# Second mixer of a two-layer diffusion trunk: the chunk states are stepped group by group inside the input projection, whose column tiles come in another order

## The reference: what is computed

```python
proj = h @ in_w                                   # 1024 x (2048 + 3072 + 64)
z = proj[..., :SSD_D_INNER]
xbc = jax.nn.silu(_dwconv(proj[..., SSD_D_INNER:SSD_D_INNER + SSD_XBC], conv_w, conv_b))
dt_raw = proj[..., SSD_D_INNER + SSD_XBC:]
...
chunk_states = jnp.einsum('bcsgn,bcsgrp->bcgrpn', bm, xdt * decay_end[..., None])
...
def step(s, inp):
    st, dec = inp
    return s * dec[..., None, None] + st, s
```

## Time and profile before

| | |
|---|---|
| median of 3 runs | 3976.86 us (3973.53 to 3977.45) |
| the profiled execution | 3977.04 us, its span 3975.4 us |
| busy share | PE 88%, weight loads 74%, DVE 46%, ACT 32%, POOL 11% |
| dt projection done, rates begin | 1880.5 us from the span's start |
| last matmul of the projection | 2400.1 us |
| first transfer of the stage of its own | 2417.8 us |
| first transfer of the scan | 2568.8 us |

### The profile page before, as it was taken

The page is one execution under the profiler, slowest core; times in us unless marked ns, Lnnn a source line. Parts: engine busy times, 40 slices in busy tenths (PEclk is TensorE's granted clock), DMA queues, the critical chain, the costliest instruction groups (busy, mean ns, idle before and its releaser), DMA issues. The chain is left out here.

```text
span 3975.4 us, 58612 instructions
## 1 busy us (share of the span) xinstructions
PE 3486.9 (88%) x23815; PEld 2930.3 (74%) x23815; DVE 1821.3 (46%) x2973; ACT 1286.6 (32%) x2031; POOL 435.2 (11%) x411
## 2 busy tenths in 40 slices
PE   4999798978599999995999995679997499999995
PEld 2999543457599999994999994345554499999994
DVE  6233456455433333334204553778885533333332
ACT  4222302024132333334113332156664123333222
POOL 0000000000111111110000112400000011111121
PEclk6999898989799999996999997789997599999997
DMA  6566302154688788863222227786664478887884
GB/s 223 181 199 205 125 0 71 44 185 140 246 291 288 277 291 294 288 235 99 91 84 68 83 68 222 271 307 223 223 228 157 172 277 289 294 290 279 295 294 166
DMA packets 381736, 801.33 MB, mean 202 GB/s; under 512 B 20663, under 2 KB 65404, under 8 KB 380171
## 3 DMA queue, kind: packets, MB, share of 16 engines
q1 hardware_dynamic: 348876, 710.85, 50.6%
q0 software_dynamic: 28368, 86.61, 7.4%
q10 hardware_dynamic: 4368, 2.20, 0.3%
HBM read 690.69 MB, written 108.90 MB: 201 GB/s over the span
## 5 line engine op out<-in xcount | busy, mean ns | idle before, releaser
L2016 PEld LDWEIGHTS moe_banks<-moe_xt,mix_ring 128*128 128x128 f32 x8192 | 1012.1, 191 | 5.5 <-issue 3.2
L2016 PE MATMUL moe_banks<-moe_xt,mix_ring 128*128 128x144 f32 x8192 | 1013.4, 287 | 3.1 <-ACT moe_xt L2051 3.1
L62 PE MATMUL ssdin_banks<-h_leading,ssdin_w_split 128*128 128x384 f32 x1920 | 386.1, 336 | 5.8 <-ACT ssdin_pad L2320 2.9
L2038 PE MATMUL moe_banks<-moe_down_parts,moe_hid_parts 128*128 128x512 f32 x1536 | 357.5, 392 | 0.0
L62 PEld LDWEIGHTS ssdin_banks<-h_leading,ssdin_w_split 128*128 128x128 f32 x1920 | 337.3, 188 | 7.2 <-issue 7.2
L2096 DVE TENSOR_TENSOR moe_hid<-moe_banks,moe_sg 128x128 f32<-128x128 f32 x256 | 74.6, 292 | 580.7 <-ACT moe_sg L2074 580.7
L2038 PEld LDWEIGHTS moe_banks<-moe_down_parts,moe_hid_parts 128*128 128x128 f32 x1536 | 285.8, 188 | 71.4 <-issue 13.2
L2086 DVE TENSOR_TENSOR moe_down_parts<-mix_ring,moe_down_parts 128x2048 fp32r<-128x2048 f32 x128 | 292.3, 2283 | 0.0
L1983 POOL DMA_INDIRECT x_dram<-moe_yc,mix_idx_quarter x128 | 167.5, 1308 | 1089.3 <-DVE moe_yc L2107 1027.0
L2872 PE MATMUL scan_banks<-scan_w,scan_yc 128*128 128x512 f32 x576 | 255.9, 598 | 0.0
L62 PE MATMUL hyin_banks<-h_leading,hyin_w_split 128*128 128x384 f32 x1152 | 237.9, 338 | 11.5 <-DVE hyin_w_split L751 11.5
(11 more groups left out here) (413 smaller groups left out, 4445.4 us busy)
## 6 DMA issues: line engine op xcount, KB each, us to landing
mix_ring<-in_moe_w_gate SPq DMA_DIRECT2D x64, 2048.0 KB, 8.0
mix_ring<-in_moe_w_up SPq DMA_DIRECT2D x64, 2048.0 KB, 12.9
mix_ring<-in_moe_w_down SPq DMA_DIRECT2D x64, 2048.0 KB, 17.3
early_ring<-in_ada_w SPq DMA_DIRECT2D x96, 512.0 KB, 6.1
scan_cum<-row_dram SPq DMA_DIRECT2D x36, 1024.0 KB, 6.2
ssd_w<-in_ssd_in_w SPq DMA_DIRECT2D x10, 2048.0 KB, 9.3
scan_states<-s_dram SPq DMA_DIRECT2D x36, 512.0 KB, 7.7
s_dram<-st_state SPq DMA_DIRECT2D x16, 1024.0 KB, 10.0
```

Of the source, the lines that this page charges most:

```text
L62: ins = pe.matmul(out(piece), w_at(w[a], k), h_k(h[b], k, piece), start=(k == 0 and a == 0 and b == 0), stop=(k == KD - 1 and a == 1))
L2016: ins = pe.matmul(pb[:, 2 * (f % 2) + j, 0:SLOTS], ring[:, 2 * half + j, k, col:col + P], xt[:, k, :], start=(k == 0), stop=(k == KD - 1))
L2038: ins = pe.matmul(pb[:, LAT_BANK[half], :], hid_parts[:, a, k, :], wd[:, half, b, k, :], start=(k == 0 and a + b == 0), stop=(k == KD - 1 ...
```

## The change

`phase_states` is gone. The projection's tiles come in another order: three z tiles (q = 0 to 2), then four periods of nine, one for each group g: B (j = 0), four x tiles (j = 1 to 4), four z tiles (j = 5 to 8); in the last period C tiles take the place of three z tiles, and the fourth C tile comes last (q = 39). Each tile's 72 matmuls are cut in two halves, and small pieces of other work, called units, stand on PE behind each half (`middle`, `end`): turns of the tile before, of the initial states, and from j = 6 on two steps of both directions a tile. Units take turns in the two banks 6 and 7 that the projection leaves free. x and B are turned from SBUF, not read back. The decays are on DVE. The rates' turns and sums are spread over tiles 1 to 4. Every loop is written out; weights are loaded one tile at a time in a ring of three. The buffers of the softplus are reused for rows and states (`work`). Rows and states are stored by SP in pieces of one group. SP, ACT, PE, DVE and POOL have one program each, as before.

```diff
-def product3(pe, out, w, w_at, h, h_k):
...
+    for k in ks:
...
+TILES_IN = 40
+LEAD_IN = 3
+PERIOD = 9
+STEPS = 7
+CTX_SLOT = 7
...
+def place(q):
+    return divmod(q - LEAD_IN, PERIOD)
+def xbc_tile_of(q):
+    if q < LEAD_IN:
+        return None
+    g, j = place(q)
+    if g == GROUPS:
+        return Z_TILES + 2 * GROUPS - 1
+    if j == 0:
+        return Z_TILES + g
+    if j <= 4:
+        return 4 * g + j - 1
+    if g == GROUPS - 1 and j >= 6:
+        return Z_TILES + GROUPS + j - 6
+    return None
+def z_tile_of(q):
+    return q if q < LEAD_IN else LEAD_IN + 4 * place(q)[0] + place(q)[1] - 5
+def tile_columns(q):
+    x = xbc_tile_of(q)
+    at = z_tile_of(q) * P if x is None else INNER + x * P
...
+def ssd_weight(sp, io, keep, q):
+    win = io["ssd_in_w"][0].rearrange("(k p) n -> p k n", p=P)
+    sp.dma_start(keep["ssd_w"][:, q % SSD_RING, :, :], win[:, :, tile_columns(q)]).then_inc(keep["s_ssd_w"][q % SSD_RING], 16)
...
+U_TURN, U_LAST, U_DECAY, U_ROWS, U_GROUP, GROUP_UNITS = 0, 2, 3, 9, 12, 33
+U_B, U_X, U_INIT, U_STEP = 0, (3, 7, 11, 14), (6, 10), 17
...
+        xrow = work[:, 0:TILES * GW].rearrange("p (t c) -> p t c", c=GW)
+        state = work[:, TILES * GW:TILES * GW + 4 * GW].rearrange("p (d b c) -> p d b c", d=2, b=2)
         ROW_PARTS = ((0, 4), (4, 8), (8, 9))
+        PARTS = ((1, 5), (5, 9), (0, 1))
...
+        def side(u):
+            return pb[:, 6 + u % 2, :]
+        def wait_empty(eng, u):
+            if u >= 2:
+                eng.wait_ge(s_side[u % 2], u // 2)
...
+                def keep_step(g, i):
+                    for d in range(2):
+                        wait_taken(sp, step_unit(g, i, d))
+                        sp.dma_start(io["s_dram"][2 + i if d == FWD else 7 - i, :, g, d, :], state[:, d, (i + 1) % 2, :]
+                                     ).then_inc(s_kept[d][(i + 1) % 2], 16)
...
+                load_init(0)
+                load(SSD_RING)
+                load(SSD_RING + 1)
+                for q in range(TILES_IN):
+                    if q >= LEAD_IN:
+                        g, j = place(q)
+                        if 3 <= j <= 4:
+                            keep_init(g, j - 3)
+                        if j == 5 and g + 1 < GROUPS:
+                            load_init(g + 1)
+                        if j == 6:
+                            keep_rows(g)
+                        if j >= 6:
+                            keep_step(g, 2 * (j - 6))
+                            keep_step(g, 2 * (j - 6) + 1)
+                        if j == 0 and g:
+                            keep_step(g - 1, 6)
+                            keep_ctx(g - 1)
...
+                def turn(q, u, part):
+                    pe.wait_ge(s_si, XBC_BEFORE[q] + 1)
+                    wait_empty(pe, u)
+                    for n, c in enumerate(range(*PARTS[part])):
+                        ins = pe.transpose(side(u)[:, n * P:(n + 1) * P], out[:, q % 2, columns(c)], ident)
+                    ins.then_inc(s_unit, 1)
...
+                def contribute(g, s):
+                    if s == 0:
+                        for part in range(3):
+                            wait_taken(pe, unit(g, U_B + part))
+                    for d in range(2):
+                        u = step_unit(g, s, d)
+                        b_rows = brow[:, chunk_of(s, d), :]
+                        pe.wait_ge(s_xw, 16 * g + 2 * s + d + 1)
+                        wait_empty(pe, u)
+                        if s == CTX_SLOT:
+                            for j in range(4):
+                                ins = pe.matmul(side(u)[:, j * P:(j + 1) * P], xw[:, d, j * P:(j + 1) * P], b_rows,
+                                                start=True, stop=True)
+                        else:
+                            ins = pe.matmul(side(u), b_rows, xw[:, d, :], start=True, stop=True)
+                        ins.then_inc(s_unit, 1)
...
+                def middle(q):
+                    if q == 2:
+                        turn_last()
+                    if q == 3:
+                        cumulate(2)
+                        cumulate(3)
+                    if q == 4:
+                        for n in range(3):
+                            cumulate_rows(n)
+                    if q <= LEAD_IN:
+                        return
+                    g, j = place(q)
+                    if j == 2:
+                        turn(q - 2, unit(g, U_B + 2), 2)
+                    if 3 <= j <= 6:
+                        turn(q - 2, unit(g, U_X[j - 3] + 2), 2)
+                    if 3 <= j <= 4:
+                        turn_init(g, j - 3)
+                    if j >= 6:
+                        contribute(g, 2 * (j - 6))
+                    if j == 0:
+                        contribute(g - 1, 6)
...
+                for q in range(TILES_IN):
+                    if q == 1:
+                        pe.wait_ge(s_dv, 1)
+                    project(q, 0)
+                    middle(q)
+                    project(q, 1)
+                    end(q)
...
+                for q in range(TILES_IN):
+                    if xbc_tile_of(q) is None:
+                        z_tile(q)
...
+                        xbc_tile(q)
+                    end(q)
+                    lead(q + 2)
+                    if xbc_tile_of(q) is not None:
+                        silu(q)
+                    middle(q + 1)
...
+                def decay(g, i, d):
+                    now, nxt = i % 2, (i + 1) % 2
+                    c = chunk_of(i, d)
+                    if i == 0:
+                        wait_taken(dve, unit(g, U_INIT[d]))
                     else:
+                        wait_taken(dve, step_unit(g, i - 1, d))
+                    if 4 * g + (i + 1) // 2:
+                        dve.wait_ge(s_kept[d][nxt], 16 * (4 * g + (i + 1) // 2))
+                    h0 = d * HEADS + g * GH
+                    dve.tensor_tensor(by_head(state[:, d, nxt, :]), by_head(state[:, d, now, :]),
+                                      per_head(rates[:, c, R_TOT, h0:h0 + GH]), ALU.mult).then_inc(s_dec, 1)
...
+                def slot(g, s):
+                    for d in range(2):
+                        add(g, s, d)
+                    for d in range(2):
+                        weigh(g, s + 1, d)
+                    if s + 1 < STEPS:
+                        for d in range(2):
+                            decay(g, s + 1, d)
...
+                for q in range(TILES_IN):
+                    end(q)
+                    if xbc_tile_of(q) is not None:
+                        taps(q)
+                    rest(q + 2)
+                    if q >= LEAD_IN and place(q)[1] == 5:
+                        for d in range(2):
+                            decay(place(q)[0], 0, d)
+                        for d in range(2):
+                            weigh(place(q)[0], 0, d)
+                    middle(q + 1)
...
-def phase_states(nc, io, keep):
...
-                keep["ssd_w"] = early.sb("w", [P, 2, KD, HALF])
+                keep["ssd_w"] = early.sb("w", [P, SSD_RING, KD, P])
...
-            phase_states(nc, io, keep)```

How the order moves on two engines. On PE, at the end of the projection and in the stage behind it, before (st_xb is x and B read back, tri holds the identity, st_xw the weighted rows, st_brow the rows of B):

```order
L62 MATMUL ssdin_banks<-h_leading,ssdin_w_split 128x384 x3
L2258 REGISTER_ALU
L2258 COMPARE_AND_BRANCH
L2201 UNCONDITIONAL_BRANCH
L2593 UNCONDITIONAL_BRANCH
L2603 MATMUL st_banks<-tri,st_xb 128x128 x20
L2612 MATMUL st_banks<-tri,st_init 128x128 x16
...
L2630 MATMUL st_banks<-st_xw,st_brow 128x512 x8
L2627 MATMUL st_banks<-st_brow,st_xw 128x128 x32
```

More of the change, by code:

```diff
@@ L2188, in phase_ssd_in @@
         s_st = [m.sem(f"stored{b}") for b in range(2)]
[L2189 to L2192, removed]
+        s_rates = m.sem("rates_rows")
+        s_rw = m.sem("weights_ready")
         s_cr = m.sem("cumulated_rows_stored")
[L2194 to L2195 removed]
+        s_unit = m.sem("side_unit_done")
+        s_side = [m.sem(f"side_bank_emptied{b}") for b in range(2)]
@@ new lines, in step_unit, with chunk_of, chunk_part, columns @@
+        def step_unit(g, s, d):
+            return unit(g, U_STEP + 2 * s + d)
+        def chunk_of(s, d):
+            if s == CTX_SLOT:
+                return 0
+            return 1 + s if d == FWD else 8 - s
+        def chunk_part(c):
+            return 2 if c == 0 else (c - 1) // 4
+        def columns(c):
+            return slice(0, P) if c == 0 else slice(LAT_AT + (c - 1) * P, LAT_AT + c * P)
+        def wait_out_free(act, q):
+            if q >= 2:
+                act.wait_ge(s_st[q % 2], STORED_BEFORE[q])
+            if q >= 2 + LEAD_IN:
+                g, j = place(q - 2)
+                if j == 0 and g < GROUPS:
+                    act.wait_ge(s_unit, unit(g, U_B + 2) + 1)
+                elif 1 <= j <= 4:
+                    act.wait_ge(s_unit, unit(g, U_X[j - 1] + 2) + 1)
@@ L2250, in _ @@
```

(42 more changed lines are left out.)

703 lines of the change are left out of this document (302 added, 401 removed).

## The result

The changed kernel takes 3889.37 us (median of 4 runs, 3889.2 to 3890.54), the kernel before 3976.97 in the same session (3973.53 to 3977.45): ratio 0.9781, 95% interval 0.9769 to 0.9793. That is 87.6 us less; forecast were 67, with 3893 as the lowest time of the range. The direction held, the size did not.

A forecast was written before the change was run, and what follows sets the result against it. The prediction took TensorE's matmuls to bound the projection, with no engine filling the stage behind it. Its terms summed to 620.8 us against 688.3, 67.5 us less: 3910 us from 3976.9, range 3893 to 3942.

The forecast's parts named there:

- interruptions: In the projection, 73 places where other matmuls break the stream, 0.2 us each: 14.6 us.
- rival (a): In the projection, interruptions are free: 14.6 us less, 3895; chance 0.1.
- Context: Context matmuls in the projection, 24 ahead of the last tile's end at an upper price of 0.28 us: 6.8 us.
- Steps: State steps added to TensorE in the projection, 56 at 0.88 us: 49.3 us.
- Turns: Turns added to TensorE in the projection, 212 over four groups at 0.109 us: 23.1 us.
- Rates: Turns, sums and rows of the rates in the projection: 7.1 us, plus a 2 us stall at the third rows.
- DVE in the last group: In the last group's C tiles, taps leave DVE the thinnest cover; TensorE waits 1 us.
- The tail: From the last projection matmul to the next stage's first transfer: 17.7 us, unchanged.
- (b): In the projection, interruptions cost more or handovers stall: at 0.6 us a place 29 us more, 3939; chance 0.2.
- (c): In the steps, state stores set the pace from landings of 14.7 us; at 22 us 4012; chance 0.06.
- (d): DVE or the clock holds the projection throughout: no change, 3977; chance 0.02.
- What would show it: Profile signs: last projection matmul near 2483 us, scan near 2501, two-step tiles 16.4 us apart, TensorE waits under 15 us.

The follow-up runs named there:

- the doubled turns: Changed kernel with every turn of x and B made twice, 180 more turns in the same breaks: 3908.33 us.
- slower weightings: Changed kernel with the 56 decays moved back from DVE to POOL: 3894.81 us.
- the pair of lone and blocked turns: Changed kernel plus 80 turns of a constant block, singly in 80 breaks: 3901.62 us; in 10 blocks of 8: 3898.36 us.
- both behind the tile: Changed kernel with all small pieces of a tile behind its last matmul, none in its middle: 3923.15 us.

## Why the prediction missed

**The step that failed** is the term "interruptions", 73 x 0.2 = 14.6 us, and with it the chance of 0.1 for rival (a). Measured: 0.01 to 0.02 us a place. M of the changed kernel, refilled with distances between starts: 38 tiles x 12.48 = 474.2, turns 23.1, steps 56 x 0.858 = 48.0 (0.429 from one record to the next in the kernel before), context 3 x 1.8 = 5.4, rates with their wait and their own breaks 8.3, together 559.0 of 560.51. What is left, 1.5 us, is what the 67 other breaks cost, 0.02 each. The 0.19 us was read rightly from the earlier trace rows, but it belongs to the change to narrow matmuls and back, whose price was then measured at 0.34 us. Every unit of this change but the rates' is in the projection's own wide form. The rows of the rates show the gap still (1905.80 instead of 1905.70, and 0.62 us on return); its price was in the earlier trace rows already.

**The other terms** by the trace after, 17.7 us in all under the sum of 620.8 (from ACT's first instruction behind the dt projection the stretch took 2484.08 - 1880.94 = 603.1):
- Interruptions: 1.5 for 14.6, 13.1 less.
- Context: 5.4 for 6.8, 1.4 less. The upper price had a low clock in it, as was said. A block of 8 takes (2336.38 - 2333.54 - 1.04) = 1.80 us.
- Steps: 48.0 for 49.3, 1.3 less. The 6.17 us of the earlier trace rows hold the tail of the last matmul too (7 x 0.858 are 6.0). Turns: 23.1, as predicted; the doubled turns confirm the price.
- Rates: 7.1, as predicted, their stall 1.2 for 2, 0.8 less. The stall was where it was expected, at the third rows.
- DVE in the last group: no wait for 1 us, 1 less. Its place was right: extra stores and slower weightings cost time there first.
- The tail: 17.6 for 17.7, 0.1 less.

**Outside the stretch** the profiled executions differ by 2.6 us more (87.7 less 85.1); the scan and what follows took 1403.4 us against 1406.6. Kernels with the same code there took up to 1407.1, so I take it for the scatter between executions. No run shows a cause.

**The rivals.** (a) came true, but for 0.02 us a place, and is shown by the pair of lone and blocked turns; its 3895 lay 6 us above the measured time, 3 for the other terms and 3 for what lies outside the stretch. (b) is refuted at this distance of units; with both behind the tile it is what happens, for want of distance. (c) did not come: stores landed in 2.0 us, weights in 4.1. Four times the stores cost 5 us in M and 8 in the time, at landings of 4.8 us; its 14.7 us were not tested. The Trainium skill's advice to split loads and stores between issuing engines (Perfetto Trace Analysis, DMA Optimizations) and to send 1 MiB or more at once (DMA: Bandwidth & Descriptors, Rules for kernel authors) had nothing to win here: neither TensorE nor DVE waits for a transfer in the stretch. (d) is refuted.

**What would show it** came out so: TensorE busy over 97% from 1881 to 2483, at clock 1.00 up to its last matmul near 2466, waits under 15 us, decays at 0.68, stores under 12 us. The last matmul was due near 2483 and ended at 2466.5, the scan near 2501 and began at 2484.1, a two-step tile was due every 16.4 us and took 15.96: three signs of one wrong term.

## What to carry to other kernels

A stream of matmuls on a full TensorE can be interrupted for the price of what is put in, if the foreign matmuls have the stream's form and their operands are ready. A price seen at a change of form must not be taken for one at a change of source. What decides is the distance between units that need each other: half a tile here; with none, every second step waited 1.4 us. Before a gap is added to a sum, look at the weight-load rows around it for an idle time. Take a unit price from the distance between starts: a run's whole busy time divided by its number holds the tail of the last one too. A median can hide a wait; look at the lengths one by one where two engines meet.

## What was not expected of the hardware

- A change between 128 x 128 and 128 x 32 weights and back costs 0.34 us (idle 0.25 and 0.20 us in the weight loads), a change of operands in the same form 0.01 to 0.02.
- Behind one idle time on an otherwise full TensorE the clock was low: 3.75 us for 1.88 of matmuls behind 4.5 us, 3.58 us behind 2.3 us. So these waits cost 1.9 and 1.7 us more than they lasted.
- A weighting on DVE that meets a decay on POOL waits for the whole of it and ends 0.55 us behind it, 37 of 64 times; a median of 0.895 us looked like a slowdown of 0.2.
- A narrow float32 matmul with 128 columns moved takes 0.055 us where successive ones write in turn to four different sets of 32 partitions, a wide one (8 in 1.80 us) 0.225, a turn of the same size 0.109.
